# The start of a projection kernel: first weight blocks and x in halves over three queues, products block by block

## The chip, the core and the metric

The kernel runs on one core of a Trainium2 chip. The metric is the device time of one execution in microseconds. The core has five engines that run side by side and meet only at semaphores: PE (TensorE, matmuls; its weight loads are listed as PEld), DVE (VectorE), ACT (ScalarE), POOL (GpSimd) and SP (SyncE, which here only issues DMAs).

## The reference

x has 256 tokens of 2048 channels, float32. It is normalised and multiplied by one wide matrix of 18512 columns; three mixers work on the columns, and their outputs are projected, gated, summed and projected again.

```python
def reference(x, norm_g, w_in, a_ws, a_b, b_conv, p_a, p_b, p_c, w_o, rel_bias, final_g):
    L = x.shape[1]
    topk = min(TOPK_MAX, L // 4)
    for l in range(DEPTH):                       # DEPTH = 1
        h = rmsnorm(x, norm_g[l])
        proj = jnp.einsum('bsd,de->bse', h, w_in[l])
        (a_u, a_v, a_z, b_bg, b_cg, b_x, b_z, c_q, c_k, c_v, c_z,
         i_q, i_k, i_w, g_a, g_b, g_c) = split_columns(proj)
        y_a = spatial_gating(a_u, a_v, a_ws[l], a_b[l]) * jax.nn.silu(a_z)
        y_b = short_gated_conv(b_bg, b_cg, b_x, b_conv[l]) * jax.nn.silu(b_z)
        y_c = dsa_attention(c_q, c_k, c_v, i_q, i_k, i_w, rel_bias, topk) * jax.nn.silu(c_z)
        m = (jax.nn.sigmoid(g_a) * (y_a @ p_a[l])
             + jax.nn.sigmoid(g_b) * (y_b @ p_b[l])
             + jax.nn.sigmoid(g_c) * (y_c @ p_c[l]))
        x = x + m @ w_o[l]
    return rmsnorm(x, final_g)
```

## The kernel before

**Products in three terms.** Every float32 operand is split into a high part (cast to fp32r) and a low part (the rest). ACT writes the high part of a weight slot (`wh`, line 361), DVE subtracts it from the raw slot to get the low part (`wl`, line 629). The activations are split likewise into `hh` (ACT, line 389) and `hl` (DVE, line 650). A product is then hh·wh + hh·wl + hl·wh, three matmuls of 128x128 by 512 columns.

**Slots.** Weights come in slots of two k blocks (KS = 2; a k block is 128 rows of the matrix) by 512 columns, 512 KB each, in a ring of four (`raw`, `wh`, `wl`). A slot gives 12 products: 2 k blocks, 2 token tiles, 3 terms. Eight slots make a chunk of 512 columns over all 16 k blocks, summed in `acc[0]` and `acc[1]`. SP issues all weight loads; a load into a used place waits for DVE's `low_split`. ACT's cast of a slot waits for the load (`raw_loaded`) and, from slot 4 on, for `sub_used`, which PE raises when the slot that had the place is used up.

**The start.** The mean square of the rows isn't waited for: the products run on x times `norm_g`, and a factor per token, `inv`, is put in when results leave psum. For this the kernel needs x transposed. PE does that with `transpose_x(j)`, two k blocks at a time, four transposes of 128x128 into the psum areas `x_t`; ACT reads them there, scales by `g_t` and writes `hh`; DVE writes `hl` from the same area. `norm_g` itself is loaded by ACT's queue (`g_s`), transposed by PE (line 1010) and copied to `g_t` (line 383). Ahead of it stand WARM_UP = 14 transposes of the identity that nothing reads. x comes in five pieces of 256, 256, 512, 512, 512 columns (`PIECES`), all issued by SP between the weight slots. POOL builds the identity (lines 310 and 312), waits for x piece 2 and issues six small loads.

**PE's order.** Warm-up, norm_g, transposes of k blocks 0 to 3, then `first_product`: slot 0 term by term, each term over both tiles (lines 1031, 1035, 1039). Slots 1 to 7 go through `product` (lines 993 to 995), where the three terms alternate, each after a wait for the slot's `low_split` and `hl_ready`. Transposes for later k blocks stand ahead of slots 1 to 5. Behind slot 7 come 48 products of 80 rows with the columns of I_K (lines 1057 to 1059), in two slots of 640 columns.

**ACT's and DVE's order.** ACT casts slot 0, then for j = 0 to 7 writes the two `hh` of slot j, squares half a row tile (j = 3 to 6, line 379, for the mean square) and casts slot j + 1. DVE follows: `hl` of slot j, `wl` of slot j + 1. After `hl` of slot 7 DVE sums the squares (`var`, line 654), ACT takes the root, DVE the reciprocal with a correction step (lines 659 to 668), `diag` (line 672), and then `wl` of the first I_K slot.

Of the kernel before, what the change touches and what calls it, by code (L numbers as in the profile page):

```python
# [41 lines left out]
WARM_UP = 14  # L42
PIECES = [(0, 256), (256, 512), (512, 1024), (1024, 1536), (1536, 2048)]
# [45 lines left out]
def trunk(nc, x, norm_g, w_in, a_ws, a_b, b_conv, p_a, p_b, p_c, w_o, rel_bias, final_g,  # L89
# [8 lines left out]
    with ExitStack() as ctx:  # L98
# [3 lines left out]
        def sem(name):  # L102
            return ctx.enter_context(nc.semaphore(name))
# [55 lines left out]
        x_t = [psum[:, 2 + k // 2 % 6, k % 2 * SEQ:(k % 2 + 1) * SEQ] for k in range(KD)]  # L159
# [47 lines left out]
        low_split = sem("low_split")  # L207
        sub_used = sem("sub_used")
# [34 lines left out]
        def _(sp):  # L243
            def load_x(i):
                c = slice(*PIECES[i])
                sp.dma_start(x_s[:, :, c], x_v[:, :, c]).then_inc(x_loaded[i], 16)
# [62 lines left out]
        def _(pool):  # L309
# [4 lines left out]
            pool.wait_ge(x_loaded[2], 16)  # L314
# [42 lines left out]
        def _(act):  # L357
# [14 lines left out]

            act.dma_start(g_s, norm_g.rearrange("o (k c) -> (o k) c", c=P)).then_inc(g_loaded, 16)
# [10 lines left out]
            split(0, 0, 0)  # L384
            act.wait_ge(gt_ready, 1)
            for j in range(SUB):
                act.wait_ge(xt_done, j + 1)
                for k in range(KS * j, KS * j + KS):
                    act.activation(hh[:, k], x_t[k], ACT.Copy, scale=g_t[:, k:k + 1]).then_inc(hh_ready, 1)
                if j in (3, 4):  # L390
                    act.wait_ge(x_loaded[j - 1], 16)
                    square(j - 3, 0)
                if j in (5, 6):
                    act.wait_ge(x_loaded[4], 16)
                    square(j - 5, 1)
                if j < SUB - 1:
                    if j + 1 >= RING:
                        act.wait_ge(sub_used, j + 2 - RING)
                    split(j + 1, (j + 1) % RING, (j + 1) // RING)
# [225 lines left out]
        def _(dve):  # L625
# [18 lines left out]
            split(0, 0)  # L644
            dve.wait_ge(ident_ready, 2)
            dve.wait_ge(gt_ready, 1)
            for j in range(SUB):
                dve.wait_ge(hh_ready, KS * j + KS)
                for k in range(KS * j, KS * j + KS):
                    dve.scalar_tensor_tensor(hl[:, k], x_t[k], g_t[:, k:k + 1], hh[:, k].bitcast(F32),  # L650
                                             ALU.mult, ALU.subtract).then_inc(hl_ready, 1)
                if j == SUB - 1:
                    dve.wait_ge(sq_done, 2 * T)
                    dve.scalar_tensor_tensor(var, ssq[:, :, 0], EPS, ssq[:, :, 1], ALU.add, ALU.add).then_inc(var_done, 1)
                if j < SUB - 1:
                    split(j + 1, (j + 1) % RING)
# [323 lines left out]
        def _(pe):  # L980
# [29 lines left out]
            pe.transpose(bank[5][:, 0:KD], g_s, ident[0:KD, 0:KD]).then_inc(gt_done, 1)  # L1010

            def transpose_x(j):

                pe.wait_ge(x_loaded[(0, 1, 2, 2, 3, 3, 4, 4)[j]], 16)
                if j == 5:
                    pe.wait_ge(gt_ready, 1)
                if j >= 6:
                    pe.wait_ge(hl_ready, KS * (j - 6) + KS)
                for k in range(KS * j, KS * j + KS):
                    for t in range(T):  # L1020
                        mm = transpose(x_t[k][:, t * P:(t + 1) * P], x_s[:, t, k * P:(k + 1) * P])
                mm.then_inc(xt_done, 1)

            def first_product():

                w_h, w_l = (w[:, 0].rearrange("p (k c) -> p k c", k=KS) for w in (wh, wl))
                pe.wait_ge(high_split, 1)
                pe.wait_ge(hh_ready, KS)
                for j in range(KS):
                    for t in range(T):  # L1030
                        pe.matmul(acc[t], hh[:, j, t * P:(t + 1) * P], w_h[:, j], start=j == 0, stop=False)  # L1031
                pe.wait_ge(low_split, 1)
                for j in range(KS):
                    for t in range(T):
                        pe.matmul(acc[t], hh[:, j, t * P:(t + 1) * P], w_l[:, j], start=False, stop=False)
                pe.wait_ge(hl_ready, KS)
                for j in range(KS):
                    for t in range(T):
                        mm = pe.matmul(acc[t], hl[:, j, t * P:(t + 1) * P], w_h[:, j], start=False, stop=False)
                mm.then_inc(sub_used, 1)  # L1040
# [282 lines left out]
```

## Time and profile before

| | us |
|---|---|
| median of 3 runs | 1074.51 |
| lowest and highest of them | 1073.25, 1074.75 |
| the profiled execution | 1074.84 |
| its span, first to last instruction | 1073.1 |
| PE matmuls busy | 1062.9 (99%) |
| DVE, ACT, POOL busy | 605.1, 503.8, 32.4 |
| memory read | 200.55 MB, 189 GB/s over the span |

The profile is one execution. Busy times are counted from the span's start. In a timeline a row is one instruction or a run of alike ones: start, duration of the whole row, engine, line of the kernel, operation, output<-inputs, count, and in brackets how long the engine had been idle and what ended that. Matmuls are pipelined: the duration of one is longer than the distance to the next. The chain of waits, followed back from the end, gives each instruction only the distance. The share of time in which PE is busy is no measure of speed by itself, since a matmul at the lower clock is busy too, for longer.

### The profile page before, as it was taken

The numbers are of one execution on the slowest core, as the hardware profiler recorded it, in microseconds if no ns is written. First come the engines' busy times: TensorE is split into PE (matmuls) and PEld (weight loads), VectorE is DVE, ScalarE is ACT, GpSimd is POOL, SyncE is SP. The second block draws the span as 40 slices with busy tenths as digits, with TensorE's granted clock in tenths as the row PEclk, the third lists the DMA queues.
The fourth block names the chain that finished last, engine by engine and source line by source line (L and its number), as shares of the span: only waits on it lengthen the run. The fifth ranks groups of instructions, "written<-read, shape, count | busy, mean of one in ns | idle before, by whom it ended". The sixth has DMA issues, their size and how long they took to land.

```text
span 1073.1 us, 14461 instructions
## 1 busy us (share of the span) xinstructions
PE 1062.9 (99%) x4880; PEld 878.6 (82%) x4880; DVE 605.1 (56%) x723; ACT 503.8 (47%) x617; POOL 32.4 (3%) x42
## 2 busy tenths in 40 slices
PE   9999999999999999999999999999999999999997
PEld 7888878888788888888888888888888888888886
DVE  5544454555576455565555575655556566666555
ACT  7444444444454444454444554444445545444443
POOL 1000000000003100000000000000000000000003
PEclk9999999999999999999999999999999999999999
DMA  9676666666666666656666656666665555566553
GB/s 290 208 215 188 188 187 184 176 179 190 176 188 190 196 194 196 187 174 179 179 179 178 177 173 180 177 180 191 180 192 177 179 194 189 183 224 228 195 195 138
DMA packets 105347, 203.14 MB, mean 189 GB/s; under 512 B 8340, under 2 KB 8896, under 8 KB 104928
## 3 DMA queue, kind: packets, MB, share of 16 engines
q1 hardware_dynamic: 104528, 200.43, 61.7%
q0 software_dynamic: 608, 1.72, 0.5%
q8 instruction: 21, 0.34, 0.1%
q10 hardware_dynamic: 176, 0.53, 0.1%
q14 instruction: 14, 0.11, 0.0%
HBM read 200.55 MB, written 2.11 MB: 189 GB/s over the span
## 4 chain that ended last, share of the span: by engine, by line
PE 98%; DVE 1%; DMA 0%; ACT 0%; issue 0%; SPq 0%; DVEq 0%; ACTq 0%
PE psum L993 31%; PE psum L995 31%; PE psum L994 31%; PE psum L1002 2%; DMA keep<-x 0%; PE psum L1139 0%; PE psum L1094 0%; PE psum L1191 0%; PE psum L1093 0%; PE psum L1057 0%; PE psum L1059 0%; PE psum L1058 0%; PE psum L1130 0%; PE psum L1131 0%; PE psum L1031 0%; PE psum L1138 0%
## 5 line engine op out<-in xcount | busy, mean ns | idle before, releaser
L629 DVE TENSOR_TENSOR wl<-raw,wh 128x1024 fp32r<-128x1024 f32 x370 | 453.9, 1227 | 436.0 <-ACT wh L361 435.4
L361 ACT CAST wh<-raw 128x1024 fp32r<-128x1024 f32 x370 | 388.6, 1051 | 531.4 <-PE psum L995 525.8
L993 PE MATMUL psum<-wh,hh 128*128 128x512 f32 x1268 | 497.8, 393 | 0.0
L995 PE MATMUL psum<-wh,hl 128*128 128x512 f32 x1268 | 494.0, 390 | 0.0
L994 PE MATMUL psum<-wl,hh 128*128 128x512 f32 x1268 | 493.6, 389 | 0.0
L995 PEld LDWEIGHTS psum<-wh,hl 128*128 128x128 f32 x1268 | 238.0, 188 | 50.4
L993 PEld LDWEIGHTS psum<-wh,hh 128*128 128x128 f32 x1268 | 238.1, 188 | 49.3 <-DVE keep L638 0.5
L994 PEld LDWEIGHTS psum<-wl,hh 128*128 128x128 f32 x1268 | 238.2, 188 | 48.2
L993 PE MATMUL psum<-wh,yh 128*128 128x512 f32 x192 | 75.1, 391 | 0.0
L995 PE MATMUL psum<-wh,yl 128*128 128x512 f32 x192 | 74.7, 389 | 0.0
L994 PE MATMUL psum<-wl,yh 128*128 128x512 f32 x192 | 74.7, 389 | 0.0
L993 PEld LDWEIGHTS psum<-wh,yh 128*128 128x128 f32 x192 | 36.0, 188 | 7.6 <-DVE yl L845 0.2
L995 PEld LDWEIGHTS psum<-wh,yl 128*128 128x128 f32 x192 | 36.0, 188 | 7.5
L994 PEld LDWEIGHTS psum<-wl,yh 128*128 128x128 f32 x192 | 36.1, 188 | 7.3
L354 POOL TENSOR_TENSOR keep<-keep 128x512 f32<-128x512 f32 x7 | 10.5, 1535 | 699.4 <-DMA keep<-final_g 699.4
L638 DVE TENSOR_SCALAR keep<-psum,stats 128x512 f32 (+1 forms) x24 | 18.0, 750 | 9.6 <-PE psum L995 9.6
L371 ACT ACTIVATE keep<-psum,stats 128x512 f32 (+1 forms) x24 | 16.5, 690 | 7.8 <-PE psum L995 7.8
L1002 PE MATMUL psum<-ident,keep 128*128 128x128 f32 x112 | 17.6, 284 | 0.8 <-DMA keep<-x 0.8
L1002 PEld LDWEIGHTS psum<-ident,keep 128*128 128x128 f32 x112 | 14.1, 146 | 3.5 <-DMA keep<-x 1.3
L569 ACT ACTIVATE keep<-keep (+1 forms) x12 | 12.7, 1054 | 0.0
L701 DVE SCALAR_TENSOR_TENSOR keep<-keep,iw 128x128 f32<-128x128 f32 (+1 forms) x32 | 11.9, 414 | 1.0
L638 DVE TENSOR_SCALAR early<-psum,stats 128x512 f32 (+1 forms) x12 | 9.0, 751 | 5.5 <-PE psum L995 5.5
(166 smaller groups left out, 390.5 us busy)
## 6 DMA issues: line engine op xcount, KB each, us to landing
raw<-w_in SPq DMA_DIRECT2D x288, 512.0 KB, 3.7
raw<-w_o SPq DMA_DIRECT2D x32, 512.0 KB, 3.7
raw<-p_c SPq DMA_DIRECT2D x16, 512.0 KB, 3.6
raw<-p_a SPq DMA_DIRECT2D x16, 512.0 KB, 4.0
raw<-p_b SPq DMA_DIRECT2D x16, 512.0 KB, 3.9
keep<-x SPq DMA_DIRECT2D x1, 2048.0 KB, 9.2
keep<-x SPq DMA_DIRECT2D x3, 512.0 KB, 9.2
keep<-bias_table POOLq DMA_DIRECT2D x1, 1024.0 KB, 7.1
```

What stands on the lines that cost most here:

```text
L354: pool.tensor_tensor(y_out[:, t, c], x_o[:, t, c], fg_all[:, c], ALU.mult).then_inc(xf_ready, 1)
L361: act.copy(wh[:, slot, 0:width], raw[:, slot, 0:width]).then_inc(high_split, 1)
L371: act.activation(dst, acc[0], ACT.Copy, scale=inv[:, 0:1]).then_inc(evac[0], 1)
L569: act.activation(here, here, ACT.Sigmoid).then_inc(sig_ready, 1)
L629: dve.tensor_tensor(wl[:, slot, 0:width], raw[:, slot, 0:width], wh[:, slot, 0:width].bitcast(F32), ALU.subtract).then_inc(low_split, 1)
L638: dve.tensor_scalar(dst, acc[1], inv[:, 1:2], None, ALU.mult).then_inc(evac[1], 1)
L701: dve.scalar_tensor_tensor(score[:, s], relu[:, h, s], iw[:, t, bass.ds(2 * i + h, 1)], score[:, s], ALU.mult, ALU.add).then_inc(score_ste ...
L993: pe.matmul(dst[t], h, w_h[:, j], start=start, stop=False)
L994: pe.matmul(dst[t], h, w_l[:, j], start=False, stop=False)
L995: mm = pe.matmul(dst[t], l, w_h[:, j], start=False, stop=stop)
L1002: return pe.transpose(dst, src, order[:])
```

## The change

- x comes in seven pieces of 128, 128, 256, 256, 256, 512 and 512 columns. Piece 0 is issued by ACT's queue ahead of `norm_g`, pieces 1 and 2 by POOL's after the identity is built, 3 to 6 by SP. POOL's small loads wait for piece 6 instead of piece 2 of five.
- Slots 0 and 1 are loaded in halves of one k block, 256 KB each, first on SP's queue. `first_loaded` counts the first halves, `raw_loaded` the second.
- 9 warm-up transposes stand ahead of norm_g's transpose and 2 behind it.
- `transpose_x(k)` does one k block (two transposes), and each k block has its own psum bank among six.
- For k blocks 0 to 3 ACT casts half a slot and writes one `hh`, in turn; DVE does the same with `wl` and `hl`; PE multiplies one k block at a time (`early_product` with count 1, six products), and after each stands the transpose of k block k + 2.
- From slot 2 on ACT writes the two `hh` of slot j first and then casts slot j; DVE writes `hl` of slot j and then `wl` of slot j. PE goes term by term through `early_product`, with waits of its own ahead of hh·wh, hh·wl and hl·wh. The squares stand behind the casts of slots 4 to 7, `var` behind `wl` of slot 7.

```diff
-WARM_UP = 14
-PIECES = [(0, 256), (256, 512), (512, 1024), (1024, 1536), (1536, 2048)]
+WARM_UP = 9
+WARM_MORE = 2
+PIECES = [(0, 128), (128, 256), (256, 512), (512, 768), (768, 1024), (1024, 1536), (1536, 2048)]
+FINE = 2
...
-        x_t = [psum[:, 2 + k // 2 % 6, k % 2 * SEQ:(k % 2 + 1) * SEQ] for k in range(KD)]
+        x_t = [psum[:, 2 + k % 6, k // 6 % 2 * SEQ:(k // 6 % 2 + 1) * SEQ] for k in range(KD)]
...
-            load_first(0)
-            load_x(0)
-            load_x(1)
-            load_first(1)
-            load_x(2)
+            for g in range(FINE):
+                for k in range(KS):
+                    sp.dma_start(raw[:, g, k * N:(k + 1) * N],
+                                 w_in_v[:, KS * g + k, C_Z:C_Z + N]).then_inc(raw_loaded[g] if k else first_loaded[g], 16)
+            load_x(3)
             load_first(2)
+            load_x(4)
             load_first(3)
-            load_x(3)
-            load_x(4)
+            load_x(5)
+            load_x(6)
...
-            pool.wait_ge(x_loaded[2], 16)
+            for i in (1, 2):
+                c = slice(*PIECES[i])
+                pool.dma_start(x_s[:, :, c], x_v[:, :, c]).then_inc(x_loaded[i], 16)
+            pool.wait_ge(x_loaded[6], 16)
...
+            act.dma_start(x_s[:, :, slice(*PIECES[0])], x_v[:, :, slice(*PIECES[0])]).then_inc(x_loaded[0], 16)
             act.dma_start(g_s, norm_g.rearrange("o (k c) -> (o k) c", c=P)).then_inc(g_loaded, 16)
...
+            for k in range(FINE * KS):
+                g, i = k // KS, k % KS
+                half = slice(i * N, (i + 1) * N)
+                act.wait_ge(raw_loaded[g] if i else first_loaded[g], 16)
+                act.copy(wh[:, g, half], raw[:, g, half]).then_inc(high_split if i else first_high, 1)
+                high_x(k)
+            for j in range(FINE, SUB):
                 for k in range(KS * j, KS * j + KS):
...
+                    high_x(k)
+                if j >= RING:
+                    act.wait_ge(sub_used, j + 1 - RING)
+                split(j, j % RING, j // RING)
+                if j == 4:
...
+            for i in range(WARM_MORE):
+                transpose(bank[4][:, 0:P], ident[:])
...
+            def early_product(k0, count, slot, wait, last=False):
...
+                pe.wait_ge(*high)
+                for j in range(count):
+                    pe.wait_ge(hh_ready, k0 + j + 1)
                     for t in range(T):
...
+                        pe.matmul(acc[t], hh[:, k0 + j, tok[t]], w_h[:, j], start=k0 + j == 0, stop=False)
+                pe.wait_ge(*low)
...
             transpose_x(0)
             transpose_x(1)
-            first_product()
-            for g in range(1, SUB):
-                for j in {1: (2, 3), 2: (4,), 3: (5,), 4: (6,), 5: (7,)}.get(g, ()):
-                    transpose_x(j)
-                pe.wait_ge(hl_ready, KS * g + KS)
-                product(g, g % RING, g, g == SUB - 1, hh, hl, KS * g, 0)
+            for k in range(FINE * KS):
+                g, i = k // KS, k % KS
+                mm = early_product(k, 1, g, ((high_split, g + 1), (low_split, g + 1)) if i else ((first_high, g + 1), (first_low, g + 1)))
+                if i:
+                    mm.then_inc(sub_used, 1)
+                transpose_x(k + 2)
+            transpose_x(FINE * KS + 2)
+            transpose_x(FINE * KS + 3)
+            for g in range(FINE, SUB):
+                early_product(KS * g, KS, g % RING, ((high_split, g + 1), (low_split, g + 1)), last=g == SUB - 1).then_inc(sub_used, 1)
+                for k in range(KS * (g + 2), min(KS * (g + 3), KD)):
+                    transpose_x(k)
```

The order of instructions on PE from the first transposes of x to the end of slot 0, before (`keep` holds x, `wh`, `wl`, `hh`, `hl` are the split operands):

```order
L1002 MATMUL psum<-ident,keep 128x128 [waits x_loaded0]
L1002 MATMUL psum<-ident,keep 128x128 x3
L1002 MATMUL psum<-ident,keep 128x128 [waits x_loaded1]
L1002 MATMUL psum<-ident,keep 128x128 x3
L1031 MATMUL psum<-wh,hh 128x512 [waits hh_ready,high_split]
L1031 MATMUL psum<-wh,hh 128x512 x3
L1035 MATMUL psum<-wl,hh 128x512 [waits low_split]
```

The same place after the change, up to the transpose of k block 2:

```order
L1029 MATMUL psum<-ident,keep 128x128 [waits x_loaded0]
L1029 MATMUL psum<-ident,keep 128x128
L1029 MATMUL psum<-ident,keep 128x128 [waits x_loaded1]
L1029 MATMUL psum<-ident,keep 128x128
L1061 MATMUL psum<-wh,hh 128x512 [waits hh_ready,first_high]
L1061 MATMUL psum<-wh,hh 128x512
L1065 MATMUL psum<-wl,hh 128x512 [waits first_low]
L1065 MATMUL psum<-wl,hh 128x512
L1069 MATMUL psum<-wh,hl 128x512 [waits hl_ready]
L1069 MATMUL psum<-wh,hl 128x512
L1029 MATMUL psum<-ident,keep 128x128 [waits x_loaded2]
```

Four transposes instead of eight stand ahead of the first product, and a transpose stands between every six products.

PE after the change, from the end of k block 3 to the products of slot 2:

```order
L1069 MATMUL psum<-wh,hl 128x512 [waits hl_ready]
L1069 MATMUL psum<-wh,hl 128x512
L1029 MATMUL psum<-ident,keep 128x128 [waits gt_ready,x_loaded3]
L1029 MATMUL psum<-ident,keep 128x128
L1029 MATMUL psum<-ident,keep 128x128 [waits hl_ready,x_loaded4]
L1029 MATMUL psum<-ident,keep 128x128
L1029 MATMUL psum<-ident,keep 128x128 [waits hl_ready,x_loaded4]
L1029 MATMUL psum<-ident,keep 128x128
L1061 MATMUL psum<-wh,hh 128x512 [waits hh_ready,high_split]
```

ACT from the cast of slot 1 to that of slot 3, before:

```order
L361 CAST wh<-raw 128x1024 [waits raw_loaded1]
L389 ACTIVATE hh<-psum,early 128x256 [waits xt_done]
L389 ACTIVATE hh<-psum,early 128x256
L361 CAST wh<-raw 128x1024 [waits raw_loaded2]
L389 ACTIVATE hh<-psum,early 128x256 [waits xt_done]
L389 ACTIVATE hh<-psum,early 128x256
L361 CAST wh<-raw 128x1024 [waits raw_loaded3]
```

The same place after; the row with x3 is hh of k blocks 3, 4 and 5, each with a wait of its own:

```order
L403 CAST wh<-raw 128x512 [waits first_loaded1]
L397 ACTIVATE hh<-psum,early 128x256 [waits xt_done]
L403 CAST wh<-raw 128x512 [waits raw_loaded1]
L397 ACTIVATE hh<-psum,early 128x256 [waits xt_done] x3
L369 CAST wh<-raw 128x1024 [waits raw_loaded2]
L397 ACTIVATE hh<-psum,early 128x256 [waits xt_done] x2
L369 CAST wh<-raw 128x1024 [waits raw_loaded3]
```

The cast of slot 2 stood ahead of hh 4 and 5, which belong to it; now it stands behind them.

## Rows read from the trace of the kernel before

**Rows 1.** The page: span, and busy time of the engines.

```profile
span 1073.1 us, 14461 instructions
...
PE 1062.9 (99%) x4880; PEld 878.6 (82%) x4880; DVE 605.1 (56%) x723; ACT 503.8 (47%) x617; POOL 32.4 (3%) x42
```

**Rows 2.** Busy time by stretch, PE alone: from:to, length, busy (count), granted clock, DMA share, GB/s.

```profile
0.00:12.21 12.21, 9.86 (x37) 1.00 0.84 276
12.21:34.14 21.93, 21.93 (x110) 1.00 0.85 268
```

**Rows 3.** The chain of waits, 0 to 20 us: start, us, what.

```profile
8.04 1.78 PE psum L1031 x4
9.83 1.46 PE psum L1035 x4
11.28 0.92 PE psum L1039 x4
...
13.08 0.23 PE psum L993
...
15.82 0.44 PE psum L1002 x4
```

**Rows 4.** Timeline of PE (its rows of the first 13 us).

```profile
1.60 3.25 PE L1002 MATMUL psum<-ident 128*128 128x128 f32 x14 [1.60 <-POOL ident L312]
...
5.58 1.12 PE L1002 MATMUL psum<-ident,keep 128*128 128x128 f32 x4 [0.52 <-DMA keep<-x]
6.93 1.12 PE L1002 MATMUL psum<-ident,keep 128*128 128x128 f32 x4 [0.23 <-DMA keep<-x]
7.78 2.04 PE L1031 MATMUL psum<-wh,hh 128*128 128x512 f32 x4
...
12.04 1.04 PE L1002 MATMUL psum<-ident,keep 128*128 128x128 f32 x8
```

**Rows 5.** Lines 1031 and 1039, to 13 us: count, duration ns min/median/max, first and last start.

```profile
L1031 PE MATMUL psum<-wh,hh x4: 628/628/764, 7.8 to 9.2; 128*128 128x512 f32 x4
...
L1039 PE MATMUL psum<-wh,hl x4: 387/392/397, 11.1 to 11.8; 128*128 128x512 f32 x4
```

**Rows 6.** DMA issues in three windows: queue, count, KB each, us from issue to landing.

```profile
raw<-w_in SPq DMA_DIRECT2D x1, 512.0 KB, 4.0
early<-norm_g ACTq DMA_DIRECT2D x1, 8.0 KB, 2.3
...
early<-rel_bias POOLq DMA_DIRECT2D x1, 1.0 KB, 5.2
...
bias_table<-early POOLq DMA_DIRECT2D x1, 12.0 KB, 3.2
```

**Rows 7.** Timeline: the issue of norm_g, and the end of POOL's first work.

```profile
0.81 0.46 ACTq L373 DMA_DIRECT2D early<-norm_g  x1
...
1.25 0.29 POOL L312 TENSOR_SCALAR_AFFINE_SELECT ident<-ident 128x128 f32<-128x128 f32 x1 [0.23 <-POOL ident L310]
```

**Rows 8.** Groups by form, 0 to 40 us, of ACT and of DVE: busy us, mean ns.

```profile
L361 ACT CAST wh<-raw 128x640 fp32r<-128x640 f32 x2 | 1.3, 718 | 0.0
...
L629 DVE TENSOR_TENSOR wl<-raw,wh 128x640 fp32r<-128x640 f32 x2 | 1.6, 818 | 0.0
```

**Rows 9.** Timeline of ACT and DVE, slots 2 and 3.

```profile
11.30 1.05 ACT L361 CAST wh<-raw 128x1024 fp32r<-128x1024 f32 x1 [1.06 <-DMA raw<-w_in]
...
12.38 1.23 DVE L629 TENSOR_TENSOR wl<-raw,wh 128x1024 fp32r<-128x1024 f32 x1 [0.83 <-ACT wh L361]
...
12.68 0.84 ACT L389 ACTIVATE hh<-psum,early 128x256 fp32r<-128x256 f32 x2 [0.33 <-PE psum L1002]
...
13.41 1.05 ACT L361 CAST wh<-raw 128x1024 fp32r<-128x1024 f32 x1
```

**Rows 10.** Timeline of DVE, from the sum of squares to the first I_K slot.

```profile
28.32 0.15 DVE L654 SCALAR_TENSOR_TENSOR stats<-stats 128x2 f32<-128x2 f32 x1
...
30.14 1.55 DVE L629 TENSOR_TENSOR wl<-raw,wh 128x640 fp32r<-128x640 f32 x2
```

More of the change, by code:

```diff
@@ L207, in trunk @@
         low_split = sem("low_split")
+        first_loaded = [sem(f"first_loaded{g}") for g in range(FINE)]
+        first_high, first_low = sem("first_high"), sem("first_low")
         sub_used = sem("sub_used")
@@ L383, in _, with high_x @@
             act.copy(g_t, bank[5][:, 0:KD]).then_inc(gt_ready, 1)
-            split(0, 0, 0)
             act.wait_ge(gt_ready, 1)
-            for j in range(SUB):
-                act.wait_ge(xt_done, j + 1)
-                for k in range(KS * j, KS * j + KS):
[L389 to L393, printed above, removed]
-                    act.wait_ge(x_loaded[4], 16)
[L395 to L399, printed above, removed]
+            def high_x(k):
+                act.wait_ge(xt_done, k + 1)
+                act.activation(hh[:, k], x_t[k], ACT.Copy, scale=g_t[:, k:k + 1]).then_inc(hh_ready, 1)
+            for k in range(FINE * KS):
[5 more added lines that the diff above has]
+            for j in range(FINE, SUB):
+                for k in range(KS * j, KS * j + KS):
+                    high_x(k)
[3 more added lines that the diff above has]
+                if j == 4:
+                    act.wait_ge(x_loaded[4], 16)
+                    square(0, 0)
+                if j == 5:
+                    act.wait_ge(x_loaded[6], 16)
+                    square(0, 1)
+                if j in (6, 7):
+                    square(1, j - 6)
             act.wait_ge(var_done, 1)
@@ L643, in _, with low_x @@
             dve.memset(ones, 1.0).then_inc(diag_ready, 1)
-            split(0, 0)
             dve.wait_ge(ident_ready, 2)
             dve.wait_ge(gt_ready, 1)
-            for j in range(SUB):
-                dve.wait_ge(hh_ready, KS * j + KS)
-                for k in range(KS * j, KS * j + KS):
[L650 to L656, printed above, removed]
+            def low_x(k):
+                dve.wait_ge(hh_ready, k + 1)
+                dve.scalar_tensor_tensor(hl[:, k], x_t[k], g_t[:, k:k + 1], hh[:, k].bitcast(F32),
+                                         ALU.mult, ALU.subtract).then_inc(hl_ready, 1)
+            for k in range(FINE * KS):
+                g, i = k // KS, k % KS
+                half = slice(i * N, (i + 1) * N)
+                dve.wait_ge(*((high_split, g + 1) if i else (first_high, g + 1)))
+                dve.tensor_tensor(wl[:, g, half], raw[:, g, half], wh[:, g, half].bitcast(F32),
+                                  ALU.subtract).then_inc(low_split if i else first_low, 1)
+                low_x(k)
+            for j in range(FINE, SUB):
+                for k in range(KS * j, KS * j + KS):
+                    low_x(k)
+                split(j, j % RING)
+            dve.wait_ge(sq_done, 2 * T)
+            dve.scalar_tensor_tensor(var, ssq[:, :, 0], EPS, ssq[:, :, 1], ALU.add, ALU.add).then_inc(var_done, 1)
             dve.wait_ge(root_done, 1)
@@ L1024, in first_product @@
[L1024 to L1040, printed above, removed]
+            for i in range(WARM_MORE):
+                transpose(bank[4][:, 0:P], ident[:])
@@ new lines, in transpose_x @@
+            def transpose_x(k):
+                pe.wait_ge(x_loaded[(0, 1, 2, 2, 3, 3, 4, 4, 5, 5, 5, 5, 6, 6, 6, 6)[k]], 16)
+                if k == 5:
+                    pe.wait_ge(gt_ready, 1)
+                if k >= 6:
+                    pe.wait_ge(hl_ready, k - 5)
+                for t in range(T):
+                    mm = transpose(x_t[k][:, t * P:(t + 1) * P], x_s[:, t, k * P:(k + 1) * P])
+                mm.then_inc(xt_done, 1)
+            def early_product(k0, count, slot, wait, last=False):
+                w_h, w_l = (w[:, slot].rearrange("p (k c) -> p k c", k=KS)[:, k0 % KS:k0 % KS + count] for w in (wh, wl))
+                high, low = wait
+                tok = [slice(t * P, (t + 1) * P) for t in range(T)]
+                pe.wait_ge(*high)
+                for j in range(count):
+                    pe.wait_ge(hh_ready, k0 + j + 1)
+                    for t in range(T):
+                        pe.matmul(acc[t], hh[:, k0 + j, tok[t]], w_h[:, j], start=k0 + j == 0, stop=False)
+                pe.wait_ge(*low)
+                for t in range(T):
+                    for j in range(count):
+                        pe.matmul(acc[t], hh[:, k0 + j, tok[t]], w_l[:, j], start=False, stop=False)
+                pe.wait_ge(hl_ready, k0 + count)
+                for t in range(T):
+                    for j in range(count):
+                        mm = pe.matmul(acc[t], hl[:, k0 + j, tok[t]], w_h[:, j], start=False, stop=last and j == count - 1)
+                    if last and t == 0:
+                        mm.then_inc(tile0_done, 1)
+                return mm
@@ L1042, in _ @@
             transpose_x(0)
             transpose_x(1)
[L1044 to L1049 removed]
+            for k in range(FINE * KS):
+                g, i = k // KS, k % KS
+                mm = early_product(k, 1, g, ((high_split, g + 1), (low_split, g + 1)) if i else ((first_high, g + 1), (first_low, g + 1)))
+                if i:
+                    mm.then_inc(sub_used, 1)
+                transpose_x(k + 2)
```

8 lines of the change are left out of this document (removed).

## The prediction

> **What bounds the kernel now.** The page comes first: TensorE's matmuls are busy for 1062.9 of 1073.1 us [rows 1]. The busy time by stretch says where the other 10 us lie: after 12.21 us PE is busy for 21.93 of 21.93 us, in the first 12.21 us only for 9.86 [rows 2]. So from 12.21 us on the end of the kernel is a count of matmuls, and a change of the first steps is worth what it moves in one quantity, PE's **lost time**: the moment from which PE never waits again, less the work done by then at full rate. Full rate is read from the chain of waits: 0.23 us for a product of 512 columns, 0.44 for four transposes (0.11 each) [rows 3]. By 12.21 us PE has done 12 products (2.76) and 8 transposes of x (0.88), so 12.21 - 3.64 = 8.6 us are lost.
>
> What they consist of is in PE's timeline. 14 warm-up transposes fill 1.60 to 4.85; then PE waits for x, 0.52 us before piece 0 and 0.23 before piece 1 [rows 4]. The first product starts at 7.78, when the second four transposes are through. So 7.78 - 0.88 = 6.9 us are lost by then. The rest is the clock: the chain gives 1.78, 1.46 and 0.92 us to three groups of four equal products [rows 3], and one product takes 628 ns in the first group and 392 in the third [rows 5]. Those are the lower (1.2 GHz) and upper (2.4 GHz) of PE's two levels, changing in the middle of the second group, some 3 us after the first product. The granted clock is no guide here: it prints 1.00 for the whole stretch [rows 2]. 4.16 us for 12 products instead of 2.76: 1.4 us. The sum is 8.3 of the 8.6; handovers are the rest.
>
> **The change, part by part.**
>
> Warm-up and g. Nine warm-ups of 0.232 us (3.25 by 14 [rows 4]) end at 3.7. norm_g landed 2.3 us after its issue at 0.81 [rows 6, 7]; now it is issued some 0.46 later behind 128 KB of x. I put it at 4.2: not before 3.6 (only the later issue), hardly after 4.9 (a 512 KB weight block issued at the same time took 4.0 us [rows 6]). The transpose of norm_g, two more warm-ups (0.46) and the two transposes of piece 0 (0.46 at the lower level) end at 5.2. ACT then has g_t at 4.6, casts half a block until 5.3 and writes hh 0 by 5.9. A half cast is put at 0.61 us, on the line from 0.72 us (640 columns) to 1.05 (1024) [rows 8, 9].
>
> The second x piece is the point. PE transposes it before the first product, and it now comes by GpSimd's queue, whose engine is free at 1.54 [rows 7]. Two rows bound the price: 12 KB to bias_table landed 3.2 us after issue with idle queues, 1 KB of rel_bias took 5.2 with full queues [rows 6]. The queues are filling at 1.5 us, and 128 KB have to share them, so I take 4.7: x piece 1 lands at 6.2, between 5.0 and 7.1. With two transposes (0.46) the first product starts at 6.7, with four transposes behind it: 6.7 - 0.44 = 6.26 lost instead of 6.9. **Gain 0.64 us**, between -0.2 and 1.4 (hh 0 at 5.9 is the floor).
>
> The Trainium skill prices such a transfer otherwise ("DMA: Bandwidth & Descriptors", "Anatomy of one DMA"): about 2.0 us plus the bytes at 436 GB/s, an estimate of 2.3 us for 128 KB. By it piece 1 would land before 4 us and the gain would be the whole 1.4; both transfers of POOL's queue [rows 6], longer with fewer bytes, speak against it.
>
> Clock. If the low level again lasts some 3 us from the first product, its cost of 1.4 us stays: **0**. Bounds: -1.4 (already up at the first product), and above as in the second rival.
>
> Pieces of weights, 256 KB each, and the fine order for k blocks 0 to 3: nothing on the path. Every k block's six products are 1.4 us at full rate, its half cast, hh, half wl and hl fit beside them. Raw data is ahead as well: total bytes up to slot 2 are 2.25 MB instead of 2.5, which landed in time for ACT at 11.30 [rows 9]. The later start of the small loads (after x piece 6) is hidden: PE reads them only behind the I_K products. The other order of terms within a slot changes no count. The spread of x_t over other psum banks costs nothing.
>
> **The order of ACT from slot 2 on** is what I expect to cost. Before, ACT cast slot j+1 right after the hh of slot j, so wh and wl lay ready before PE's transposes for that slot. Now ACT writes hh 4 and hh 5 first and casts slot 2 only then, and hh 5 needs the transpose that PE does after product 3. Counted from the end of product 3: transpose 5 takes 0.22; ACT sees it 0.20 later (the first four of the eight transposes at 12.04 are through at 12.48, ACT starts at 12.68 [rows 4, 9]); hh 5 holds ACT for 0.36 (a pair is spaced 0.73 from the next row [rows 9]); the cast takes 1.05; the handover 0.06: 1.89. PE has meanwhile transposes 5, 6, 7: 0.66. **PE waits 1.23.** Then four products with wh (0.91) are too short a cover for wl, 1.23 long [rows 9] with 0.06 of handover: **0.38 more.** Nothing removes these 1.61 us when x or weights come earlier, since the chain starts at PE's own product 3. From slot 4 on the transposes run a slot ahead: wl is ready 0.2 + 0.73 + 1.05 + 1.23 = 3.2 us after them, and PE wants it after a slot (2.74), four transposes (0.44) and four products (0.91), 4.1. That fits.
>
> The norm chain moves too. The last square stands behind the cast of slot 7, and var behind its wl. From transpose 14: 0.2, hh pair 0.73, cast 1.05, wl 1.13, then var to the end of the first 640-column wl as before (28.32 to 30.14 + 0.82 = 2.64 [rows 8, 10]): 5.75. PE has one transposed block and 24 products, 5.69, before it wants that wl. With handovers **0.2**, between 0 and 0.5. Before, var was written at 28.32, five us ahead of PE.
>
> Sum: -0.64 + 0 + 1.61 + 0.2 = +1.17 us. The profiled execution took 1074.84 (span 1073.1), so it would take 1076.0. The median of the three runs, 1074.51, is 0.3 below; the spread, 1073.25 to 1074.75, fits a clock that comes up at different points of the first 12 us. I stay with 1076.0.
>
> **Rivals.** A measurement of this kernel can tell 0.2%, 2.15 us, from no change: faster is below 1072.4, slower above 1076.7.
>
> First, the early start carries. Piece 1 lands at 5 us or the clock is up at the first product: -0.6 to -1.4 on the sum, with the wait for slot 2 still there: about 1074.9. For it: the low end of the queue price, and that norm_g needed 2.3 us only. Chance 0.17. The Trainium skill's figure for the transfer, above, would put it here.
>
> Second, slower: the low level lasts longer. PE's activity before the first product is thinner: 11 warm-ups instead of 14, a wait of 0.5 us for g and of 1.0 for x piece 1. Each product at the low level costs 0.2 us more. From 4 products more than forecast (0.8 us) it is over 1076.7; eight give 1077.6, and if all 24 products of blocks 0 to 3 run low it is +3, 1079. For it: 3.25 us of packed warm-ups and eight transposes didn't bring the level up before. Against it: for just that reason fewer of them may cost nothing, since what preceded the rise was the products. Chance 0.2. The Trainium skill ("TensorE: Matmul & The Clock Gate", Part 4) goes further: a transpose doesn't count as activity as a matmul does. The trace so far agrees; by that rule the shorter warm-up is free, and this case would be nearer 0.1.
>
> Third, the change doesn't do what it says: GpSimd's transfer takes the 5.2 us of rel_bias and its 128 KB on top. Piece 1 at 7.1 to 7.4, first product at 7.7, gain 0 to -0.2, and the waits behind are paid in full: 1076.8. Chance 0.12.
>
> Fourth, faster by over 0.2%: start at 5.9 (-1.4), the clock up at once (-1.4) and no wait at slot 2, because ACT gets transpose 5 sooner than I count it: 1072.0. Chance 0.04.
>
> **The numbers.** The forecast, 1075.2 to 1076.9, has 0.47. The range from 1074.1 to 1078.0 takes in the first and third, and the nearer half of the second. Faster 0.04 (the fourth); slower 0.3 (0.18 of the second, 0.08 of the third, 0.04 of the forecast's tail); the rest, 0.66, is within 0.2%.
>
> **What would show it.** In PE's timeline: first product near 6.7, after a wait of about 1 us for x piece 1; matmuls of 600 ns until some 3 us later; a gap of 1.2 us before the first product of slot 2, released by ACT's wh, and one of 0.4 before its wl; at most 0.5 before the 80-row matmuls of I_K. ACT's list: hh 5, then the 1024-column cast. I am wrong if that gap is missing, if PE's timeline shows waits for raw data instead, or if the level comes up before the first product.

## The result and the profile after

The changed kernel is slower.

| | before | after |
|---|---|---|
| median of 7 runs, us | 1074.38 | 1078.07 |
| lowest and highest | 1073.19, 1074.75 | 1076.88, 1079.49 |
| the profiled execution, its span | 1074.84, 1073.1 | 1078.01, 1076.0 |

The ratio is 1.0036, with a 95% interval from 1.0027 to 1.0045. The forecast was 1076.0, within 0.2% of before, in a range from 1074.1 to 1078.0. The change was slower instead, by more than the 0.2% that the forecast allowed, and the time lies just above the range.

The page of the kernel after says as little as that of before [rows 1] where the time went:

```profile
span 1076.0 us, 14473 instructions
...
PE 1063.4 (99%) x4877; PEld 877.9 (82%) x4877; DVE 605.7 (56%) x725; ACT 504.4 (47%) x619; POOL 33.9 (3%) x44
```

PE is busy for 0.5 us more and the span is 2.9 longer. A fixed point behind the start tells more: the transposes of the small loads (x8 in the chain of waits), behind which both kernels run the same code. In the chain of before they begin at

```profile
40.40 1.02 PE psum L1002 x8
```

and in that of after at

```profile
43.37 1.02 PE psum L1029 x8
```

So 2.97 us arise before this point, and nothing behind it. PE's own waits up to 45 us (engine, line and who was waited for: us, times, longest) name three that can differ:

```profile
PE psum L1037 <- DMA early<-norm_g: 1.7, 1, 1.7
...
PE psum L1061 <- ACT wh L369: 1.1, 1, 1.1
PE psum L1029 <- DMA keep<-x: 0.4, 1, 0.4
```

The timeline shows them in place. These are rows of PE, ACT and DVE; line 1029 transposes, 1061, 1065 and 1069 are hh·wh, hh·wl and hl·wh, 397 is hh, 369 the 1024-column cast, 648 its wl. They answer to [rows 4, 9].

```profile
5.51 0.28 PE L1037 MATMUL psum<-ident,early 16*128 16x16 f32 x1 [1.73 <-DMA early<-norm_g]
...
6.20 0.63 PE L1029 MATMUL psum<-ident,keep 128*128 128x128 f32 x2
...
7.25 0.69 PE L1029 MATMUL psum<-ident,keep 128*128 128x128 f32 x2 [0.42 <-DMA keep<-x]
...
7.59 1.20 PE L1061 MATMUL psum<-wh,hh 128*128 128x512 f32 x2
...
16.06 0.82 PE L1029 MATMUL psum<-ident,keep 128*128 128x128 f32 x6
...
16.48 0.47 ACT L397 ACTIVATE hh<-psum,early 128x256 fp32r<-128x256 f32 x1 [1.13 <-PE psum L1029]
...
16.85 1.03 ACT L369 CAST wh<-raw 128x1024 fp32r<-128x1024 f32 x1
...
17.92 1.23 DVE L648 TENSOR_TENSOR wl<-raw,wh 128x1024 fp32r<-128x1024 f32 x1 [0.45 <-ACT wh L369]
17.94 1.19 PE L1061 MATMUL psum<-wh,hh 128*128 128x512 f32 x4 [1.06 <-ACT wh L369]
...
19.20 1.19 PE L1065 MATMUL psum<-wl,hh 128*128 128x512 f32 x4
```

The first product starts at 7.59 us, 0.2 earlier than before (7.78), with four transposes less behind it. Slot 2 comes as counted: three k blocks transposed from 16.06 on, hh 5 at 16.48, the cast at 16.85, and PE's next product at 17.94. 17.94 - 16.06 - 0.66 is a wait of 1.22 us. Then 1.26 us pass from the first term to the second where four products take 0.91: 0.35 more.

The chain of waits gives the clock, as [rows 3] did:

```profile
7.94 0.85 PE psum L1061 x2
8.80 0.85 PE psum L1065 x2
9.65 0.85 PE psum L1069 x2
10.50 0.43 PE psum L1029 x2
10.93 0.85 PE psum L1061 x2
11.78 0.77 PE psum L1065 x2
12.55 0.47 PE psum L1069 x2
```

Two products in 0.85 us are the lower level, in 0.47 the upper. The rise falls into the row at 11.78, 4 to 5 us after the first product; before it came after 3. The 12 products here take 4.64 us instead of 2.76, and two transposes 0.43 instead of 0.22: 2.1 us lost to the level instead of 1.4. This is one execution. By the same count the level cost 1.5 to 2.5 us in the profiles of the other kernels below that keep the change's three queues, so the 0.7 us between 2.1 and 1.4 could as well be 0.1 or 1.1 in another execution.

### The profile page after: what moved, and what is told of

It is laid out like the page before. It is cut to its first block, busy times and chain, and to the rows that moved or that the text cites. A ratio compares the mean times of both kernels' runs of the same rounds, so it can differ in the third digit from the quotient of the medians.

```text
span 1076.0 us, 14473 instructions
## 1 busy us (share of the span) xinstructions
PE 1063.4 (99%) x4877; PEld 877.9 (82%) x4877; DVE 605.7 (56%) x725; ACT 504.4 (47%) x619; POOL 33.9 (3%) x44
## 4 chain that ended last, share of the span: by engine, by line
PE 98%; DVE 1%; DMA 1%; ACT 0%; issue 0%; POOL 0%; POOLq 0%; DVEq 0%; ACTq 0%
PE psum L1020 30%; PE psum L1022 30%; PE psum L1021 30%; PE psum L1029 2%; PE psum L1065 1%; PE psum L1069 1%; PE psum L1061 1%; DMA keep<-x 1%; PE psum L1177 0%; PE psum L1132 0%; PE psum L1229 0%; PE psum L1131 0%; PE psum L1095 0%; PE psum L1096 0%; PE psum L1097 0%; PE psum L1168 0%
## 5 line engine op out<-in xcount | busy, mean ns | idle before, releaser
L648 DVE TENSOR_TENSOR wl<-raw,wh 128x1024 fp32r<-128x1024 f32 (+1 forms) x368 | 451.3, 1227 | 425.9 <-ACT wh L369 425.4
L369 ACT CAST wh<-raw 128x1024 fp32r<-128x1024 f32 (+1 forms) x368 | 386.4, 1051 | 527.1 <-PE psum L1022 523.6
L1020 PE MATMUL psum<-wh,hh 128*128 128x512 f32 x1240 | 486.4, 392 | 0.0
L1022 PE MATMUL psum<-wh,hl 128*128 128x512 f32 x1240 | 483.0, 390 | 0.0
L1021 PE MATMUL psum<-wl,hh 128*128 128x512 f32 x1240 | 482.7, 389 | 0.0
L1022 PEld LDWEIGHTS psum<-wh,hl 128*128 128x128 f32 x1240 | 232.7, 188 | 49.0
L1020 PEld LDWEIGHTS psum<-wh,hh 128*128 128x128 f32 x1240 | 232.8, 188 | 48.5 <-DVE keep L657 0.5
L1021 PEld LDWEIGHTS psum<-wl,hh 128*128 128x128 f32 x1240 | 232.9, 188 | 47.3
```

The lines of the kernel that those rows point to most:

```text
L369: act.copy(wh[:, slot, 0:width], raw[:, slot, 0:width]).then_inc(high_split, 1)
L648: dve.tensor_tensor(wl[:, slot, 0:width], raw[:, slot, 0:width], wh[:, slot, 0:width].bitcast(F32), ALU.subtract).then_inc(low_split, 1)
L1020: pe.matmul(dst[t], h, w_h[:, j], start=start, stop=False)
L1021: pe.matmul(dst[t], h, w_l[:, j], start=False, stop=False)
L1022: mm = pe.matmul(dst[t], l, w_h[:, j], start=False, stop=stop)
```

## The experiments

Each was timed in 5 rounds beside the kernel before, a_hold in 3. "Gain" is against the changed kernel's median of 1078.07, which was measured before these runs and not again beside them. Against the kernel before in the same runs every distance can be taken too: the changed kernel is 3.7 us behind it.

**1. The order of slots 2 to 7 put back.**

```diff
+            split(FINE, FINE % RING, 0)
             for j in range(FINE, SUB):
                 for k in range(KS * j, KS * j + KS):
                     high_x(k)
...
-                split(j, j % RING, j // RING)
+                if j < SUB - 1:
+                    if j + 1 >= RING:
+                        act.wait_ge(sub_used, j + 2 - RING)
+                    split(j + 1, (j + 1) % RING, (j + 1) // RING)
```

> The changed kernel with one part undone: from slot 2 on ACT casts slot j+1 right after hh of slot j again, DVE follows, and squares and var stand where they stood before. Theory (order): the waits of 1.1 and 0.3 us at slot 2 and 0.2 us before the I_K products vanish; 1.5 us faster than the changed kernel, some 2.2 us slower than the kernel before. Rival (clock or data): PE waits there for something else as soon as ACT is early, the gain is under 0.5 us.

Measured: 1076.22 (1075.51 to 1077.85; before 1074.12), a gain of 1.85 us against 1.5 expected; ratio to before 1.0020 (1.0011 to 1.0029). It is 2.1 us behind the kernel before, which makes the gain 1.6 by that measure. In the chain of waits the three transposed k blocks and slot 2 now follow each other without a gap:

```profile
15.70 0.66 PE psum L1031 x6
16.36 0.92 PE psum L1063 x4
17.28 0.93 PE psum L1067 x4
```

The wait was ACT's order and nothing else. No wait for data took its place, and the one before the I_K products is gone as well.

**2. x pieces 0 to 2 back on SP's queue.**

```diff
             for g in range(FINE):
                 for k in range(KS):
                     sp.dma_start(raw[:, g, k * N:(k + 1) * N], ...
+                    if g == 0:
+                        load_x(k)
+                    elif k == 0:
+                        load_x(2)
...
-            for i in (1, 2):
-                c = slice(*PIECES[i])
-                pool.dma_start(x_s[:, :, c], x_v[:, :, c]).then_inc(x_loaded[i], 16)
...
-            act.dma_start(x_s[:, :, slice(*PIECES[0])], x_v[:, :, slice(*PIECES[0])]).then_inc(x_loaded[0], 16)
```

> The changed kernel with x pieces 0, 1 and 2 issued by SP between the halves of slots 0 and 1, norm_g alone on ACT's queue. Theory (queues): norm_g lands at 3.1 us instead of 5.5, x piece 1 near 5.5 instead of 7.2, the first product starts at 6.2 to 6.5 instead of 7.6, and 1.1 to 1.4 us are gained against the changed kernel. Rival: pieces of 128 columns behind the weights land no earlier on this queue, gain under 0.3 us. The wait of 1.1 us at slot 2 stays by both.

Measured: 1076.29 (1074.60 to 1077.19), gain 1.78 us. The mechanism was half right. Piece 1 went out at 2.25 and landed after 4.4 us, at 6.7, not at 5.5; the first product started at 7.07, 0.5 earlier than in the changed kernel, not 1.2. PE's waits show slot 2's unchanged and all of the wait for x in one piece:

```profile
PE psum L1029 <- DMA keep<-x: 1.7, 1, 1.7
...
PE psum L1061 <- ACT wh L370: 1.1, 1, 1.1
```

By the distance to before the gain is 1.5 us. Besides the 0.5 us there are 0.25 us outside the span (below) and, in the two profiles, 0.7 us less at the lower level (1.4 instead of 2.1).

**3 and 4. The warm-up alone**, 14 transposes in the changed kernel (`WARM_UP = 14`, a_warm14) and 9 in the kernel before (`WARM_UP = 9`, b_warm9).

> The changed kernel with 14 warm-up transposes ahead of norm_g instead of 9 (the two behind it stay). They end at 4.85 us, before norm_g lands at 5.5, so PE's start isn't delayed. Theory (thin warm-up): the clock comes up earlier, as in the kernel before, 0.9 us or more faster than the changed kernel. Rival (transposes don't count): within 0.3 us of the changed kernel.

> The kernel before with 9 warm-up transposes instead of 14. PE waits for x piece 0 at 5.6 us in both. Theory (thin warm-up): the clock comes up later, 0.5 to 1.5 us slower than before. Rival (transposes don't count): within 0.3 us of before.

Measured: a_warm14 1078.11 (1075.89 to 1079.17), gain nil. b_warm9 1074.79 (1073.93 to 1075.56) against 1074.12: 0.7 us slower by the medians, ratio 1.0008 (0.9999 to 1.0017), so not certain. The first fits the rival, the second the theory, so neither explains both; and b_warm9's profiled execution, 1073.93, was the fastest of its eleven, so its rows can't show the difference. What the warm-up does is in the stretches of a_warm14's profile (busy time of PE, PEld, DVE, ACT, POOL, then granted clock):

```profile
0.00:4.30 4.30, 2.70 (x13) 2.71 (x14) 0.16 (x2) 1.49 (x2) 2.31 (x8) 1.00 0.52 154
4.30:7.70 3.40, 1.29 (x9) 0.79 (x8) 1.12 (x3) 1.67 (x4) 0.00 (x0) 1.00 1.01 303
7.70:11.10 3.40, 3.40 (x11) 2.71 (x12) 1.74 (x3) 0.98 (x2) 0.00 (x0) 0.50 1.01 370
11.10:14.00 2.90, 2.90 (x15) 2.33 (x14) 1.66 (x3) 1.46 (x3) 0.00 (x0) 0.99 1.05 397
```

The clock was at the lower level, 0.50, from 7.70 to 11.10, and was back at the upper in the next stretch. The 1.00 of the first two rows proves nothing by itself, as it didn't in [rows 2], but the lengths of the transposes do:

```profile
5.78 0.38 PE L1029 MATMUL psum<-ident,keep 128*128 128x128 f32 x2
7.57 0.59 PE L1029 MATMUL psum<-ident,keep 128*128 128x128 f32 x2 [1.41 <-DMA keep<-x]
```

Two transposes took 0.38 us before the wait and 0.59 behind it (two transposes at the upper level take 0.38 at 12.42 us, too, and 0.63 at the lower level at 10.52). So the change at 7.7 is a fall. Until then only transposes had run, from 4.3 to 7.7 PE had waited for most of the time (1.29 of 3.40 us busy), and the products that began at 7.81 found the level just gone. The 14 packed warm-ups had brought the level up, and it was lost over the waits for norm_g (0.7 us) and x piece 1 (1.4).

**5. All of it put back but the halves**: order, queues and 14 + 2 warm-ups.

> The changed kernel with the order of slots 2 to 7, the queues of x pieces 0 to 2 and the 14 warm-ups of the kernel before; what stays of the change are the halves of slots 0 and 1, seven pieces of x and the products by k block and by term. Theory (order and queues are all that costs; each gave 1.8 us alone): 1074.3 us, within 0.4 of the kernel before, since the first product comes 0.6 us earlier but the clock decides the rest. Rival (the halves are worth their 0.6 us of earlier start): 1073.5. Rival (they cost, by more instructions and waits): over 1074.8.

Measured: 1073.23 (1072.89 to 1074.94; before 1074.08), 4.8 us better than the changed kernel, which is more than 1.85 + 1.78 + 0; ratio to before 0.9996 (0.9987 to 1.0005). The theory that order and queues are all that costs, 1074.3, missed by 1.1 us; the rival of 1073.5 is nearer. The first product starts at 6.48 and is at the upper level at once, two in 0.45 to 0.50:

```profile
6.24 0.44 PE psum L1031 x2
6.68 0.50 PE psum L1063 x2
7.18 0.45 PE psum L1067 x2
```

Seven of the eleven runs lay at 1072.9 to 1073.3 and four at 1074.5 to 1074.9. The distance, some 1.6 us, is about what the lower level cost in the kernel before (1.4). No profile of the slower four was taken, so that it is the clock is not shown.

**6. The same with 9 + 2 warm-ups.**

> As a_order_queues_warm, but with the change's 9 + 2 warm-ups instead of 14 + 2. With the change's own queues five warm-ups more made no difference (1078.11 against 1078.07). Theory (warm-ups count only where no wait of some 1 to 2 us stands between them and the first product): here that wait is shorter with 14 (0.4 us) than with 9 (1.7 us in a_queues), so 9 cost 0.8 to 1.2 us: 1074.2. Rival (warm-ups never matter): 1073.2, as with 14.

Measured: 1074.17 (1072.88 to 1075.11; before 1074.30), 0.9 us slower than with 14 by the medians, 0.7 by the distances to before. In its profile, with a wait of 1.3 us for x, the first product ran at the lower level. Here the warm-up seems to count, where in 3 it didn't. The intervals of the two kernels overlap, so the theory has support, not proof.

**7, 8 and 9. Which transfer is late, and why**: norm_g ahead of x piece 0 (a_gfirst, two lines exchanged), piece 1 on ACT's queue (a_x1_act, `act.dma_start` behind norm_g), and SP holding back slot 1 until piece 1 is there (a_hold):

```diff
             for g in range(FINE):
+                if g == 1:
+                    sp.wait_ge(x_loaded[1], 16)
```

> The changed kernel with norm_g issued ahead of x piece 0 on ACT's queue. Theory (x piece 1 by GpSimd's queue, landed at 7.2 us, is the last of what the first product waits for): norm_g lands at 3.1, the wait moves to x piece 1, the first product stays near 7.6, gain under 0.4 us. Rival (norm_g at 5.5 us is what costs): over 1 us faster than the changed kernel.

> The changed kernel with x piece 1 issued by ACT behind norm_g instead of by GpSimd, which keeps piece 2. Theory (x piece 1 is last): it lands near 6.0 us, the first product starts at 6.7 to 7.0, 0.6 to 1.2 us faster than the changed kernel. Rival: any third transfer on a busy ring lands near 7, no gain. The 2.0 us that the changed kernel's time lies above its span (1.75 before): if GpSimd's x transfers make it, it falls by half.

> The changed kernel with one wait more: SP issues the halves of slot 1, and all behind them, only when x piece 1 has landed. Theory (crowding: the 1 MB of weights issued by SP within 1.8 us shares the engines with x piece 1): piece 1 lands by 5.7 us instead of 7.2, the first product starts near 6.3, set by norm_g at the latest. Rival (latency of GpSimd's queue, 5.2 us for 1 KB in the kernel before): it lands at 6.7 or later though nothing is in its way. The time says little, since all later loads are late.

Measured: a_gfirst 1077.92 (1077.27 to 1079.52), no gain; x piece 1 took 5.8 us and the first product started at 8.01. a_x1_act 1078.73 (1078.33 to 1079.08), no gain, for which my first theory had 0.6 to 1.2. a_hold 1076.98 (1076.46 to 1077.97), 1.1 us faster. The DMA issues (us from issue to landing) of x piece 1 in the changed kernel, in a_x1_act and in a_hold, in this order:

```profile
keep<-x POOLq DMA_DIRECT2D x1, 128.0 KB, 5.4
...
keep<-x ACTq DMA_DIRECT2D x1, 128.0 KB, 5.6
...
keep<-x POOLq DMA_DIRECT2D x1, 128.0 KB, 4.3
```

ACT's queue is as slow as GpSimd's, so GpSimd's own latency isn't the cause that I had made it. With 512 KB of SP's weights held back, the same transfer on GpSimd's queue took 4.3 us, where the four kernels that issue it there without the hold had 5.4 to 5.8: crowding. It explains 1.1 us or a little more. That 4.3 remain with slot 0, x pieces 0 and 2 and norm_g beside it says that there is more, and how much of that is the queue's start isn't settled. For comparison, x pieces 0 and 1 on SP's queue with no weights issued ahead of them (a_xfirst, below):

```profile
keep<-x SPq DMA_DIRECT2D x2, 128.0 KB, 2.3
```

norm_g is another matter. It took 4.0 us in a_hold too, 4.0 to 4.1 wherever x piece 0 stood ahead of it on ACT's queue and 2.1 to 2.5 wherever it stood first, so it pays for its place and not for the weights of slot 1. In a_hold norm_g and hh 0 bind next, and the first product gains just 0.2:

```profile
5.38 0.28 PE L1039 MATMUL psum<-ident,early 16*128 16x16 f32 x1 [1.60 <-DMA early<-norm_g]
...
7.36 1.19 PE L1063 MATMUL psum<-wh,hh 128*128 128x512 f32 x2 [0.23 <-ACT hh L399]
```

That is why neither norm_g nor piece 1 gives much when it alone is moved. The 1.1 us of a_hold's median are more than these 0.2; its profiled execution, 1077.87, was nearly the slowest of the eight, and where the others gained isn't shown.

**10. The kernel before with PE's waits filled** by five more transposes of the identity that nothing reads, 2 behind norm_g's and 3 between those of x pieces 0 and 1.

> The kernel before with 2 more transposes of the identity behind norm_g's and 3 between the transposes of x pieces 0 and 1, in PE's waits for x; nothing is computed with them. Theory (transposes count, gaps undo them: the clock was up from 4.3 to 7.7 us behind 14 warm-ups in one profile and fell again over a wait): the clock is up earlier and more often at the first product, 0.4 to 1.3 us faster than before. Rival (transposes don't count): within 0.2 us, or slower by what the extra ones delay x's.

Measured: 1073.78 (1073.29 to 1074.67) against 1074.08; ratio 0.9998 (0.9989 to 1.0007). Half right. The level is up at the first product (four products in about 1 us instead of 2), but the gain is 0.3 us by the medians and not 0.4 to 1.3; profile against profile it is 1.0 at the fixed point (39.40 against 40.40). Nor does this profile show that the filling raised the level. norm_g's transpose, which stands ahead of all five, already took 0.23 us, as at the upper level in a_warm14; it took 0.28 in the kernel before, whose instructions up to there are the same. What the level is at this point varies from one execution to the next. PE now waits for the rest of the start, as its timeline shows between 10.2 and 11.65:

```profile
7.23 1.15 PE L1033 MATMUL psum<-wh,hh 128*128 128x512 f32 x4 [0.21 <-ACT hh L389]
...
10.50 1.09 PE L1002 MATMUL psum<-ident,keep 128*128 128x128 f32 x8 [0.30 <-DMA keep<-x]
11.65 0.50 PE L993 MATMUL psum<-wh,hh 128*128 128x512 f32 x1
```

The chain of waits names what it is: slot 1, landed at 8.48, then its cast, its wl and the two hl.

```profile
2.36 6.12 DMA raw<-w_in
8.51 1.06 ACT wh L361
9.59 1.22 DVE wl L629
10.81 0.80 DVE hl L650 x2
```

With 512 KB slots the slow clock hid this chain. In run 5 hardly anything is waited for there (0.1 us ahead of k block 2's transposes). That is what the halves, with the finer x pieces and products, seem to be worth; no run has the halves alone.

**11 and 12. A version that should beat both.** a_oqw_fill is run 5 with four more transposes of the identity between those of x pieces 0 and 1. a_xfirst has two there, norm_g's transpose behind 7 of 14 warm-ups, and SP's order turned to the order of need:

```diff
+                    if (g, k) == (0, 0):
+                        load_x(0)
+                        load_x(1)
+                    elif (g, k) == (1, 0):
+                        load_x(2)
                     sp.dma_start(raw[:, g, k * N:(k + 1) * N], ...
```

> As a_order_queues_warm, with 4 more transposes of the identity between those of x pieces 0 and 1, in PE's wait; nothing is computed with them. a_order_queues_warm had 7 runs at 1072.9 to 1073.3 and 4 at 1074.5 to 1074.9; its profile, of the first kind, had the clock up at 5.4 us, ahead of the first product. Theory (the second kind are runs in which the clock came up later, because of the wait): nearly all runs are of the first kind, median 1073.0. Rival (the two kinds come from something else): both stay, in like numbers.

> As a_oqw_fill, but SP issues x pieces 0 and 1 ahead of the first weight half and piece 2 ahead of the third, and norm_g's transpose stands behind 7 of the 14 warm-ups, with 2 more between x's. Theory (what must be there first should be issued first): x piece 1 lands by 5, the first product waits for hh 0 alone and starts near 6.1 instead of 6.7, 0.4 to 0.6 us faster than a_oqw_fill, about 1072.5. Rival (from the first product on, slots 1 and 2 set the pace): no gain, a wait before slot 1 or 2 takes it.

Measured: a_oqw_fill 1073.18 (1072.84 to 1075.22), ten of eleven runs below 1073.4 and one at 1075.2; ratio to before 0.9994 (0.9985 to 1.0003). The second kind of run has nearly gone, as expected of a clock that falls in a wait, though one of eleven against four of eleven can still be chance. a_xfirst 1072.99 (1072.39 to 1073.30; before 1074.30): ratio 0.9988 (0.9979 to 0.9997), 1.3 us faster than the kernel before and the only version whose interval lies below 1. None of its eleven runs is of the second kind. Its list of waits has none of PE behind the identity's, and PE's rows follow each other closely:

```profile
5.04 0.64 PE L1032 MATMUL psum<-ident,keep 128*128 128x128 f32 x2
5.47 0.63 PE L1032 MATMUL psum<-ident 128*128 128x128 f32 x2
5.90 0.55 PE L1032 MATMUL psum<-ident,keep 128*128 128x128 f32 x2
6.39 0.70 PE L1064 MATMUL psum<-wh,hh 128*128 128x512 f32 x2
```

The first product starts at 6.39, 0.5 us earlier than in a_oqw_fill (6.88), not at the expected 6.1: the first weight half, now behind x, reached ACT only for a cast at 5.25, and hh 0 came at 5.77. At the fixed point it is 0.8 us ahead of a_oqw_fill (38.08 against 38.88 us), but only 0.2 by the medians, where 0.4 to 0.6 was expected; in this profile the last stretch, behind the last matmul, was 0.6 us longer, and I didn't follow that up.

## Why the prediction was wrong

The sum was -0.64 + 0 + 1.61 + 0.2 = 1.17. Term by term, against the profiled executions, whose times differ by 3.17:

| term | forecast | measured |
|---|---|---|
| start of the first product | -0.64 | 7.59 - 0.44 = 7.15 instead of 6.9: +0.25 |
| clock | 0 | 2.1 instead of 1.4: +0.7 |
| wait at slot 2 | +1.61 | 1.22 + 0.35 = +1.57 |
| norm chain, wait before I_K | +0.2 | +0.2 |
| time outside the span | 0 | 2.0 instead of 1.75: +0.25 |

That makes 2.97; the other 0.2 have no place. The first two rows make nearly all of the error: the start 0.9 us and the clock 0.7, and the second of them rests on single executions.

**Right: the order of ACT.** The 1.23 and 0.38 us worked out from the rows of before were 1.22 and 0.35, and undoing the order gave 1.85 of the 3.7 (1.6 by the distance to before). The wait before I_K shows in the chain of after; the first small product has 0.33 us where the others have 0.12:

```profile
35.91 0.91 PE psum L1069 x4
36.82 0.33 PE psum L1095
37.15 0.12 PE psum L1096
```

**Wrong: the start.** The step that failed is "so I take 4.7: x piece 1 lands at 6.2". It took 5.4 us from its issue at 1.77, where the prediction had counted from 1.54, and landed at 7.2, just beyond the slow end of 7.1. The first product came at 7.59 instead of 6.7. norm_g was mis-sized as well: I had put it at 4.2 and "hardly after 4.9". Its row:

```profile
early<-norm_g ACTq DMA_DIRECT2D x1, 8.0 KB, 4.1
```

4.1 us from 1.32 are 5.4. Part of this was a slip: the 4.0 us of the weight block were counted from the old issue, though norm_g now goes out 0.46 later; from 1.27 they give 5.3, nearly what came. And norm_g alone would have undone the gain: in a_hold piece 1 landed at 6.1, and the first product still started at 7.36, so 6.92 us were lost, as many as before. The floor that I had put at 5.9, hh 0, lay there. The bounds came from transfers that had other traffic beside them. I had asked how long each transfer takes, and not what else SP now puts in its way: SP issues 1 MB of weights within 1.8 us, half of it not needed until k block 2, and nothing keeps the order of need any more. a_hold shows 1.1 us of it.

**Wrong: the clock as a rival of its own.** The clock's term, 0, came out at 0.7. The third rival (piece 1 late) and the second (the level stays low for longer) had 0.12 and 0.2, as if either came alone. They came together here. The third was right in its mechanism, with the first product at 7.59 for its 7.7. The prices add up: 1076.8 for the third, and 0.7 for the clock on top, is 1077.5, and the time outside the span makes it nearly 1077.8. That a wait for a late transfer can lose the level is in the rows of a_warm14. In the changed kernel itself the level wasn't up at any time before the first product (two transposes of x in 0.63 and 0.69 us), so why it rose later than before, if not by chance, stays open. The argument that fewer warm-ups may be free fits this kernel (1078.11 with 14), for a reason that I hadn't seen: in a_warm14's profile the level was up and was lost over the waits.

The Trainium skill's rule in "TensorE: Matmul & The Clock Gate", Part 4 (PE-mode transpose), that a transpose doesn't count as activity the way a matmul does, doesn't hold for the float32 transposes of this kernel if it means that they can't raise the level: it was up at the first product in run 5, two products in 0.50 us, behind nothing but transposes. The Trainium skill's price for one transfer in "DMA: Bandwidth & Descriptors", section "Anatomy of one DMA", an estimate of 2.3 us for 128 KB, was 5.4 here. The Trainium skill's rule in the same page under "Issuing engines are not separate DMA queues", that several issuing engines save only issue time, fits run 2, where x on one queue was 1.8 us faster than over three; I had left it out.

**The pieces of weights**, of which I had said "nothing on the path", are in none of the changed kernel's waits. In run 5 PE goes on at the upper level where b_dense had to wait.

## What to carry to other kernels

Spreading the first loads over several queues gives up their order: a block needed later slows the one needed first (128 KB in 5.4 us, in 4.3 with 512 KB of weights held back). One queue in the order of need was faster than three, by 1.8 us. Before a producer's work is moved behind its consumer's feed, count the chain from the consumer's last instruction to the producer's result: what PE's own work doesn't cover of it is a wait, and no earlier load takes it away. A start has one more currency than time: in a_warm14 PE's clock fell over its waits, and the products behind them ran slower, so a late transfer can cost twice and waste a warm-up. Waits of 0.4 us (run 5) and 0.6 us (a_oqw_fill) did no such harm in their profiles; the 0.7 and 1.4 us of a_warm14, one after the other, did.

## What was not expected of the hardware

- Time outside the span. The kernels whose x comes over three queues took 2.0 us more than their span (after, a_order, a_warm14, a_gfirst, a_hold: 2.00 to 2.02 in the median; a_x1_act, with two of the pieces on ACT: 2.13), all others 1.76 to 1.82, with before at 1.76. The 0.25 us don't show in any row of the profile, and what they consist of stays open.
- The lower level was left behind transposes alone (a_order_queues_warm, a_oqw_fill, b_dense), and came back in a_warm14 over a stretch with 1.29 of 3.40 us busy. It doesn't come at a fixed point: norm_g's transpose, behind the same 14 warm-ups from 1.60 on, took 0.28 us in the kernel before (lower level) and 0.23 in b_dense (upper).
- Where the rise was in the profiles, at 9 to 13.5 us in the kernels with waits, varies between kernels with nearly the same start (11.2 in a_order, 12.3 in after, 13.5 in a_x1_act). So a single profile prices the clock no better than to about 1 us.
